# State-space part of a transformer block: B and C projected in four wide blocks of 256 features, convolution taps read from SBUF, time steps transposed behind a block

## What is computed

```python
h = rms_norm(x, g_pre_mix)
q, k, v, z, xbc, dt_raw, ga, gs = _split(h @ w_in, IN_SIZES)
# ssd_branch:
xbc = causal depthwise convolution over time, 4 taps, one filter per feature (conv_w)
xbc = silu(xbc + conv_b)
xs, bm, cm = _split(xbc, (2048, 512, 512))     # x, B, C
dt = softplus(dt_raw + dt_bias)
a = -exp(a_log)
y = ssd_chunked(xh, dt, a, bm, cm)             # chunks of 128 steps, cumulative sums of dt * a
```

## Time and profile before

| | us |
|---|---|
| median of 3 runs | 1294.99 (1294.9 to 1295.42) |
| profiled execution, device time | 1295.38 |
| its span in the trace | 1294.0 |
| TensorE (PE) busy | 1275.6 (99% of the span) |
| TensorE weight loads (PEld) busy | 1100.0 (85%) |
| VectorE (DVE) busy | 978.8 (76%) |
| ScalarE (ACT) busy | 700.0 (54%) |
| GpSimd (POOL) busy | 152.5 (12%) |

### The profile page before, as it was taken

One profiled execution on the slowest core, in us unless ns is written; L12 is line 12 of the kernel. 1 busy time (PEld: TensorE's weight loads), 2 busy tenths in 40 slices (PEclk: granted clock), 3 DMA queues, 4 the chain that ended last, 5 costly groups with the idle time before them and its releaser, 6 DMA issues.

```text
span 1294.0 us, 19305 instructions
## 1 busy us (share of the span) xinstructions
PE 1275.6 (99%) x7558; PEld 1100.0 (85%) x7558; DVE 978.8 (76%) x1556; ACT 700.0 (54%) x1030; POOL 152.5 (12%) x237
## 2 busy tenths in 40 slices
PE   8999999999999999999999999999999989999999
PEld 8888899889988898888888878888888867888887
DVE  6556587978666747766667877798888887888887
ACT  5445566545545556643334755655554775655553
POOL 8000001000000001200001131000000160000000
PEclk9999999999999999999999999999999999999999
DMA  9632445423555526566665733366665612476662
GB/s 309 197 123 68 165 165 198 165 96 126 185 195 184 207 99 189 152 196 188 188 194 164 228 121 92 99 200 190 196 193 171 222 33 82 132 205 186 189 201 81
DMA packets 219705, 212.67 MB, mean 164 GB/s; under 512 B 7969, under 2 KB 177075, under 8 KB 219616
## 3 DMA queue, kind: packets, MB, share of 16 engines
q1 hardware_dynamic: 215872, 206.25, 51.2%
q0 software_dynamic: 3152, 4.15, 1.0%
q10 hardware_dynamic: 592, 1.05, 0.2%
HBM read 210.25 MB, written 1.05 MB: 163 GB/s over the span
## 4 chain that ended last, share of the span: by engine, by line
PE 89%; DVE 4%; ACT 3%; issue 2%; POOL 1%; DMA 0%; SPq 0%; ACTq 0%; DVEq 0%; POOLq 0%
PE psum_b L2351 9%; PE psum_a L2351 9%; PE psum_a L569 5%; PE psum_a L571 5%; PE psum_a L570 5%; PE psum_c L569 5%; PE psum_b L2354 5%; PE psum_c L570 5%; PE psum_a L2354 5%; PE psum_c L571 5%; PE psum_b L569 4%; PE psum_b L571 4%; PE psum_b L570 4%; PE psum_b L638 2%; PE psum_a L638 2%
## 5 line engine op out<-in xcount | busy, mean ns | idle before, releaser
L508 ACT ACTIVATE w_hi<-raw 128x2048 fp32r<-128x2048 f32 (+3 forms) x231 | 368.7, 1631 | 15.7 <-PE psum_b L2354 4.6
L518 DVE TENSOR_TENSOR w_lo<-raw,w_hi 128x2048 fp32r<-128x2048 f32 (+3 forms) x154 | 339.1, 2216 | 39.5 <-ACT w_hi L508 36.7
L2351 PE MATMUL psum_b<-x,w_hi 128*128 128x512 f32 x528 | 165.6, 395 | 0.0
L2351 PE MATMUL psum_a<-x,w_hi 128*128 128x512 f32 x522 | 164.1, 396 | 0.0
L2354 PEld LDWEIGHTS psum_b<-x,w_lo 128*128 128x128 f32 x528 | 99.2, 188 | 23.2
L531 DVE TENSOR_TENSOR w_lo<-raw,w_hi 128x512 fp32r<-128x512 f32 (+1 forms) x159 | 116.5, 736 | 2.3 <-ACT w_hi L508 2.3
L2354 PEld LDWEIGHTS psum_a<-x,w_lo 128*128 128x128 f32 x522 | 98.1, 188 | 22.8
L2507 ACT ACTIVATE ffn_pre<-ffn_both,cols 128x256 f32<-128x256 f32 x88 | 50.3, 601 | 113.1 <-DVE ffn_both L2519 113.1
L2551 POOL CAST ffn_hidden_hi<-ffn_h 128x256 fp32r<-128x256 f32 x66 | 51.1, 774 | 485.2 <-DVE ffn_h L2538 330.3
L569 PE MATMUL psum_c<-w_hi,ffn_hidden_hi 128*128 128x512 f32 x264 | 103.6, 392 | 0.6 <-DVE ffn_hidden_lo L2543 0.5
L2354 PE MATMUL psum_b<-x,w_lo 128*128 128x256 f32 x528 | 103.7, 278 | 0.0
(11 more groups left out here) (620 smaller groups left out, 2901.8 us busy)
## 6 DMA issues: line engine op xcount, KB each, us to landing
raw<-in_ffn_w_up_dram SPq DMA_DIRECT2D x88, 512.0 KB, 5.1
raw<-in_w_in_dram SPq DMA_DIRECT2D x39, 1024.0 KB, 5.3
raw<-in_w_gu_dram SPq DMA_DIRECT2D x44, 512.0 KB, 5.2
raw<-in_ffn_w_down_dram SPq DMA_DIRECT2D x44, 512.0 KB, 3.3
raw<-in_w_down_dram SPq DMA_DIRECT2D x22, 512.0 KB, 3.4
raw<-in_w_br_ssm_dram SPq DMA_DIRECT2D x8, 1024.0 KB, 5.2
raw<-in_w_xkv_dram SPq DMA_DIRECT2D x8, 1024.0 KB, 5.6
raw<-in_w_out_dram SPq DMA_DIRECT2D x8, 1024.0 KB, 5.2
```

Of the source, the lines that this page charges most:

```text
L508: act.activation(k.w_hi[:, s, 0:size], k.raw[:, s, 0:size], ACT.Copy).then_inc(*k.rounded.at(*key))
L518: dve.tensor_tensor(k.w_lo[:, s, 0:size], k.raw[:, s, 0:size], k.w_hi[:, s, 0:size].bitcast(F32), ALU.subtract).then_inc(*k.split.at(*key))
L2351: pe.matmul(ps[:, 512 * j:512 * j + 512].rearrange("p (n t) -> p n t", n=2), hi[j], k.X_both[:, :, kt, :], start=kt == 0, stop=False, skip ...
```

## The change

Four wide blocks ("bc0", 0), ("bc0", 1), ("bc1", 0), ("bc1", 1) take the place of the narrow units `bc0` and `bc1`, numbered n = 0 to 3, in psum_b, psum_a, psum_b, psum_a. Block 2 waits for VectorE's signal of block 0, block 3 for that of block 1, `xs0` for that of block 2 and `xs1` for that of block 3. Per block ScalarE copies one partial sum into a new buffer `conv_in` in SBUF, VectorE adds the other, ScalarE makes tap 3 and bias of the block's two tiles from `conv_in`, VectorE the other three taps (6 instructions) from `conv_in`. Each engine handles one weight piece between two blocks instead of two between two units. The transposes of the time steps stand behind block 0, and block 1 (whose bank held dt) also waits for VectorE's sum of dt.

```diff
+WIDE_BC = [(unit, c) for unit in ("bc0", "bc1") for c in range(2)]
...
+        self.conv_in = self.put("conv_in", [P, 4, 2, SEQ], y_lo_at)
...
         halves("dt", win, C_DT, SSM_HEADS)
-        square("bc", win, C_XBC + SSM_INNER)
+        for n, key in enumerate(WIDE_BC):
+            block(key, win, 0, KD, C_XBC + SSM_INNER + SEQ * n, SEQ)
...
-        self.before["att1", 0], self.before["bc0"] = self.before["att1"], (("att1", 0), "v")
+        self.before["att1", 0] = self.before["att1"]
+        for n, key in enumerate(WIDE_BC):
+            self.bank[key] = (self.psum_b, self.psum_a)[n % 2]
+            self.before[key] = (WIDE_BC[n - 2], "v") if n >= 2 else (("att1", 0), "v" if n == 0 else "")
+        self.before["xs0"], self.before["xs1"] = (WIDE_BC[2], "v"), (WIDE_BC[3], "v")
...
+def act_conv_wide(k, n):
+
+    act, key, (u, c) = k.nc.scalar, WIDE_BC[n], divmod(n, 2)
+    act.wait_ge(*k.used.by(*key))
+    act.activation(k.conv_in[:, n, :, :], wide_sums(k, key)[1], ACT.Copy).then_inc(*k.out_act.at(key))
+    act.wait_ge(*k.out_dve.by(key))
+    for j in range(2):
+        tile = 16 + 4 * u + 2 * c + j
+        t = act.activation(k.conv[:, u, 2 * c + j, :], k.conv_in[:, n, j, :], ACT.Identity, scale=conv_col(k, "conv_w", 3, tile),
+                           bias=conv_col(k, "conv_b", 0, tile))
+    t.then_inc(*k.conv_act.at(key))
+
+
+def act_conv_wide_silu(k, n, dst):
+    act, key, (u, c) = k.nc.scalar, WIDE_BC[n], divmod(n, 2)
+    act.wait_ge(*k.conv_dve.by(key, 3))
+    act.activation(dst[:, 2 * c:2 * c + 2, :], k.conv[:, u, 2 * c:2 * c + 2, :], ACT.Silu).then_inc(*k.conv_silu.at(f"bc{u}", c))
+
+
+def dve_conv_wide(k, n):
+    dve, key, (u, c) = k.nc.vector, WIDE_BC[n], divmod(n, 2)
+    both = k.conv_in[:, n, :, :]
+    dve.wait_ge(*k.out_act.by(key))
+    dve.tensor_tensor(both, wide_sums(k, key)[0], both, ALU.add).then_inc(*k.out_dve.at(key))
+    dve.wait_ge(*k.conv_act.by(key))
+    for d in (1, 2, 3):
+        for j in range(2):
+            out = k.conv[:, u, 2 * c + j, d:]
+            t = dve.scalar_tensor_tensor(out=out, in0=k.conv_in[:, n, j, 0:SEQ - d],
+                                         scalar=conv_col(k, "conv_w", 3 - d, 16 + 4 * u + 2 * c + j), in1=out, op0=ALU.mult, op1=ALU.add)
+        t.then_inc(*k.conv_dve.at(key, d))
+        if d < 3:
+            dve.wait_ge(*k.conv_dve.by(key, d))
...
     pe_dt(k)
-    pe_bank(k, "bc0")
-    first = turned_tiles(k, "bc0", k.X, 0)
-    take(first, 1)
-    pe_dt_turn(k)
-    take(first, 3)
-    take(turned_tiles(k, "bc0", k.X, 1), 4)
-    pe_bank(k, "bc1")
-    pe_turned(k, "bc1", k.X)
+    for n, key in enumerate(WIDE_BC):
+        pe_bank(k, key)
+        if n == 1:
+            pe.wait_ge(*k.dt_dve.by("rows"))
+        pe_wide(k, key, k.X_both)
+        if n == 0:
+            pe_dt_turn(k)
     pe_cum(k)
...
     for u, dst in ((0, k.b_t), (1, k.c_t)):
-        act_conv_first(k, f"bc{u}", u, 16 + 4 * u)
-        act_split(k)
-        act_conv_silu(k, f"bc{u}", u, dst)
+        for c in range(2):
+            act_conv_wide(k, 2 * u + c)
+            act_split(k, 1)
+        for c in range(2):
+            act_conv_wide_silu(k, 2 * u + c, dst)
...
     dve_dt(k)
     dve_split(k)
     for u in range(2):
-        dve_conv(k, f"bc{u}", u, 16 + 4 * u)
-        dve_split(k)
+        for c in range(2):
+            dve_conv_wide(k, 2 * u + c)
+            dve_split(k, 1)
```

## The result

The changed kernel takes 1298.38 us (median of 12 runs, 1297.94 to 1298.86), the kernel before 1295.46 us (12 runs beside it, 1294.66 to 1296.03): 2.9 us more, a ratio of 1.0023 with a 95% interval of 1.0016 to 1.0031. It is slower, clear of noise. The centre lies a little over the line of 0.2% that the prediction used, and the interval reaches under it.

What follows compares the result with a forecast made beforehand. TensorE, busy 99% of the span, was taken as the bound. The terms -0.76 - 0.54 + 2.6 + 1.0 + 0.1 gave +2.4 us on a median of 1294.99, so 1297.4 us, range 1296.2 to 1298.7.

Steps and rivals of the forecast that it cites:

- the line of 0.2%: Whole kernel: the smallest difference a measurement can tell from no change, 0.2% or 2.6 us.
- the main case: Whole kernel: both stalls occur, +2.4 us, with ends at 1297.0 and 1297.9 us; chance 0.68.
- case C: Ahead of xs0's transposes: ScalarE and VectorE lag over 2.0 us more, TensorE waits some 1 us; +3.4, 1298.4; chance 0.12.
- the case with 0.62 and the one with 0.36: Verdicts on the whole kernel: same within the measurable difference, chance 0.62; slower beyond it, chance 0.36.
- Part 1, the matmuls: TensorE, four blocks for four pieces: 5.57 us per block instead of 5.76 per piece wins 0.76 us.
- Part 2, the transposes: TensorE behind block 0: the transposes no longer wait for VectorE's sum of dt, which wins 0.54 us.
- Part 3, dt later: VectorE behind the moved transposes: work on dt starts 1.87 us later, delaying the rounding and splits behind it.
- Part 4, stall 1: TensorE ahead of block 2: waits 2.6 us for VectorE's add of block 0, which stands behind both splits.
- Part 4, stall 2: TensorE ahead of block 3: waits 1.0 us for the add of block 1, 6.69 us after block 0's.
- No stall ahead of xs0; part 5: xs0 avoids a stall by 0.3 us; later the lag leaves 2.0 us of slack, so the 2.4 us stay.
- The price of SBUF: VectorE's taps: reading SBUF instead of PSUM gains nothing; by the skill each would be about 65 ns shorter, sum +2.0.
- Case D, the clock: TensorE after the 2.6 us idle: clock at half for one block, 5.57 us more; +8.0, 1303.0; chance 0.04.

Runs made afterwards that it cites:

- Experiment 5: The kernel before with only the time-step transposes moved from behind bc0's first step to behind its first piece: 1294.66 us, 0.9995 of the kernel before.
- experiment 3: The changed kernel with three places in PSUM instead of two banks for dt and the four blocks: 1297.19 us, 1.0016 of the kernel before.
- experiment 6: The changed kernel with TensorE's wait ahead of block 2 lengthened on purpose, until the taps of block 0: 1303.28 us, 1.0061 of the kernel before.
- experiment 1: The changed kernel with the time-step transposes moved from behind block 0 to behind its third step of eight: 1296.23 us, 1.0006 of the kernel before.

## Why the prediction was right, and where not

The direction, the places of both stalls and their mechanism were right; 1297.4 was forecast for a kernel before of 1294.99, which is +2.4, and +2.9 was measured (+2.62 by the local count). As an absolute time 1298.38 lies above the main case (1297.0 to 1297.9); it is inside the range only through the room left for case C, a wait behind C that did not occur, and 0.47 us of it is that the kernel before came out at 1295.46. That part is luck. The likeliest case put the result just under the line of 0.2%; the ratio's centre came out just over it with an interval on both sides, so these runs do not decide between the case with 0.62 and the one with 0.36. That line was also too coarse for what was measured: the interval reaches 0.08% to either side.

- **Part 1, the matmuls (-0.76).** Held: a block without a wait takes 5.57 us (171.89 to 177.46 in the third-bank run).
- **Part 2, the transposes (-0.54).** Held but for 0.1: they begin 5.68 us after block 0 did, not 5.57. Experiment 5 measured this part alone at 0.45 to 0.58.
- **Part 3, dt later.** 1.87 forecast; 166.38 - 163.88 - 0.47 = 2.03 measured, the 0.1 of part 2 and a hand-over of 0.11 instead of 0.05. This term is what made the sum too small: the add of block 0 ends 0.19 us later than forecast, blocks 2 and 3 start on adds, and so xs0 starts at 188.08 - 0.47 = 187.61 instead of 187.4.
- **Part 4, stall 1 (2.6).** 2.42 of idle and 2.57 from start to start. The add ends at 174.42, forecast 173.76 + 0.47 = 174.23.
- **Part 4, stall 2 (1.0).** 0.83 of idle, 0.99 from start to start; the chain took 6.68 us, forecast 6.69. Tap 3 from SBUF took 1.09 and not 1.14, the taps 2.70 and not 2.66. Each block behind a stall has a slow first pair (0.73 instead of 0.63): 0.1 twice, counted once in the sum. Block 1 has one too, behind the transposes and with no stall, as the matmul behind them had before: the row from which the 0.1 was taken shows that, not a wait.
- **No stall ahead of xs0; part 5.** Right: none in the list; xs0's convolution ends at 209.00, forecast 208.5 + 0.47, and experiment 3 shows what it would cost without the 2 us that are left.
- **The price of SBUF.** The taps take 482 ns at the median from SBUF against 475 from PSUM: no gain, as the rows said and not as the Trainium skill, "VectorE: DVE Perf Modes", section "The TRN2 errata — SBUF-src ops pay a fixed extra latency per instruction", would have it.
- **Case D, the clock.** Given 0.04 and called absent at an idle of this size by the first 5 us; that step failed. The mean granted clock is under 1 in 8 of 12 executions of the changed kernel and in none of the 102 of the kernel before that ran beside the experiments. The row was not of the same kind (a kernel's start, one execution), and one profiled execution, in which the clock held, could not show it. The rule of the Trainium skill ("TensorE: Matmul & The Clock Gate", Part 1) that it is taken back after idling is what experiment 6 shows. The price was over-sized: 0.9 to 2.2 us, not 5.6, as the clock is back before the block is through (from its fifth step on in experiment 6), and nothing measurable in the changed kernel. The case's sum also left out that stall 2 (1.0 us) would take up its part of any delay: by its own terms it was +7.0, not +8.0.

The local count explains 2.6 of the 2.9 us. The other 0.3 is within what the interval leaves open (0.0016 to 0.0031 of 1295.46 us is 2.1 to 4.0 us); no run settles it.

## What to carry to other kernels

When work units are made smaller, recompute how soon each bank is wanted back against the full list that stands ahead of its read on the reading engine, not against the read itself; then put that read ahead of everything with a later due date. If more banks seem to cure a stall, ask for the rate of the chain per unit first: engines that need 6.7 us per unit of 5.6 fall behind by 1.1 us with each unit and are waited for once the slack is used up. A step that moves off TensorE's wait has a price on the engine behind it, and here a place two steps further on (2.2 us into the block, experiment 1) had the gain without the price.

## What the hardware showed that I had not expected

TensorE's clock fell to half within an idle stretch of 6.3 us and made the next block 2.2 us longer in the trace; the mean clock was lowered in all 5 executions of that kernel. With an idle of 2.4 us, or of 1.6 and 0.5 us with 1.1 us of work between them, it was lowered in some executions (8 of 12 and 13 of 22, and 4 of 11) and not in others of the same kernel, so one profiled execution cannot tell. With waits of 0.4 and 0.8 us (experiment 1) it was 1.000 in all 11. With idle matmuls in the gap it was 1.000 in 33 of 33. The loss in the executions with a lowered clock was 0.9 us behind the idle of 2.4 us, 1.8 behind the two short ones, and nothing measurable in the changed kernel, where another wait follows.
